# A two-stack transformer on one core: ten products without use after each norm's sum, present and left out

## The reference

```
def rmsnorm(x, g):
    y = xf * lax.rsqrt(jnp.mean(xf * xf, axis=-1, keepdims=True) + EPS)
    return (y * g).astype(x.dtype)

def hybrid_layer(x, ...):
    x = x + 0.5 * swiglu(rmsnorm(x, ffn1_norm), ffn1_wg, ffn1_wu, ffn1_wd)
    h = rmsnorm(x, mix_norm)
    proj = h @ w_in
    ...
    x = x + jnp.concatenate([na_o, gla_o], axis=-1) @ w_out
    x = x + 0.5 * swiglu(rmsnorm(x, ffn2_norm), ffn2_wg, ffn2_wu, ffn2_wd)
```

## Time and profile before

| | |
|---|---|
| median of three runs | 2177.46 us (2175.4 to 2190.49) |
| profiled execution, its own time | 2181.22 us |
| its span, first to last instruction | 2179.4 us |
| its mean granted TensorE clock | 0.979 of full speed |
| PE busy | 2119.0 us, 97% of the span |
| DVE busy | 1587.0 us, 73% |
| ACT busy | 1193.6 us, 55% |
| chain that ended last | PE 89%, DVE 5%, ACT 2%, DMA 2%, issue 1% |

### The profile page before, as it was taken

How to read it: one execution, slowest core, us unless ns; L and a number is a source line. 1 busy time by engine, 2 the same in 40 slices (tenths; PEclk the granted TensorE clock), 3 DMA queues, 4 the chain that set the end, 5 groups by cost and what they waited for, 6 DMA issues and landing times.

```text
span 2179.4 us, 32300 instructions
## 1 busy us (share of the span) xinstructions
PE 2119.0 (97%) x13054; PEld 1844.0 (85%) x13054; DVE 1587.0 (73%) x2592; ACT 1193.6 (55%) x2028; POOL 38.7 (2%) x38
## 2 busy tenths in 40 slices
PE   8999999999999999999899998999999999999998
PEld 7888998888888898888788896788888887668887
DVE  7887667887887576887688767588766665777665
ACT  6555565554654565655555447555455553555553
POOL 0002000000002000000000000000000000000000
PEclk9999999999999999999999997999999998799999
DMA  7886335775677533687477642287655454104543
GB/s 283 307 267 214 131 117 192 281 254 200 252 281 258 177 114 136 229 282 236 154 281 269 229 174 97 78 289 270 219 186 191 162 181 159 43 1 154 182 168 133
DMA packets 78092, 426.67 MB, mean 196 GB/s; under 512 B 9697, under 2 KB 10465, under 8 KB 47633
## 3 DMA queue, kind: packets, MB, share of 16 engines
q1 hardware_dynamic: 77968, 425.01, 55.9%
HBM read 423.93 MB, written 1.05 MB: 195 GB/s over the span
## 4 chain that ended last, share of the span: by engine, by line
PE 89%; DVE 5%; ACT 2%; DMA 2%; issue 1%; DVEq 0%; ACTq 0%
PE bank L454 40%; PE bank L458 21%; PE bank L436 5%; PE bank L438 4%; PE bank L437 4%; DVE slot_lo L1345 2%; PE bank L446 1%; PE bank L648 1%; DMA slot<-in_wd_dram 1%; PE bank L504 1%; PE bank L506 1%; PE bank L505 1%; PE bank L898 1%; DMA slot<-in_slots_dram 1%; ACT slot_hi L993 1%
## 5 line engine op out<-in xcount | busy, mean ns | idle before, releaser
L1345 DVE TENSOR_TENSOR slot_lo<-slot,slot_hi 128x1024 fp32r<-128x1024 f32 (+1 forms) x728 | 799.9, 1114 | 211.3 <-ACT slot_hi L993 210.0
L993 ACT ACTIVATE slot_hi<-slot 128x1024 fp32r<-128x1024 f32 (+1 forms) x728 | 678.3, 957 | 242.9 <-PE bank L454 110.8
L454 PE MATMUL bank<-h_both,slot_hi 128*128 128x512 f32 x2688 | 674.4, 392 | 0.0
L454 PEld LDWEIGHTS bank<-h_both,slot_hi 128*128 128x128 f32 x2688 | 483.5, 189 | 86.1
L458 PEld LDWEIGHTS bank<-h_both,slot_lo 128*128 128x128 f32 x2688 | 366.7, 190 | 26.3
L458 PE MATMUL bank<-h_both,slot_lo 128*128 128x256 f32 x2688 | 374.8, 282 | 0.0
L454 PE MATMUL bank<-act_both,slot_hi 128*128 128x512 f32 x1232 | 307.0, 395 | 0.0
L1040 ACT ACTIVATE room<-bank 128x512 f32<-128x512 f32 x176 | 105.1, 597 | 335.4 <-PE bank L454 335.3
L454 PEld LDWEIGHTS bank<-act_both,slot_hi 128*128 128x128 f32 x1232 | 223.7, 188 | 46.0
L1455 DVE TENSOR_TENSOR room<-room,bank 128x512 f32<-128x512 f32 x176 | 121.1, 688 | 149.7 <-ACT room L1040 149.7
L436 PE MATMUL bank<-h_both,slot_hi 128*128 128x256 f32 x736 | 213.7, 290 | 3.7 <-issue 1.0
(11 more groups left out here) (241 smaller groups left out, 2189.3 us busy)
## 6 DMA issues: line engine op xcount, KB each, us to landing
slot<-in_slots_dram SPq DMA_DIRECT2D x236, 1024.0 KB, 4.8
slot<-in_wd_dram SPq DMA_DIRECT2D x128, 704.0 KB, 4.1
room<-in_mod_w_dram SPq DMA_DIRECT2D x144, 512.0 KB, 4.9
room<-in_na_bias_dram SPq DMA_DIRECT2D x8, 512.0 KB, 6.1
x<-in_x_dram SPq DMA_DIRECT2D x1, 1024.0 KB, 5.3
out_dram<-h SPq DMA_DIRECT2D x4, 256.0 KB, 2.2
cond<-in_cond_dram SPq DMA_DIRECT2D x1, 512.0 KB, 9.8
room<-in_gla_mask_dram SPq DMA_DIRECT2D x1, 512.0 KB, 5.7
```

The source lines that it names most:

```text
L454: return pe.matmul(o, slot_hi[b][:, w:w + P], x_both.rearrange("p a b -> p (a b)"), start=first, stop=last)
L993: act.activation(slot_hi[b][:, c0:c1], slot[raw][:, c0:c1], ACT.Copy).then_inc(s["hi_ready"], 1)
L1345: ins = dve.tensor_tensor(slot_lo[b][:, c0:c1], slot[raw][:, c0:c1], slot_hi[b][:, c0:c1].bitcast(F32), ALU.subtract)
```

## The change

The constant `WARM` goes from 10 to 0, so `keep_warm` issues nothing. Nothing else differs: the loops of `WARM_START` and of eight products at the program's start stay.

```diff
         CONST_LOADS = 18
-        WARM = 10
+        WARM = 0
         WARM_START = 9
```

## The result

| | before | after |
|---|---|---|
| median of the runs | 2177.46 us (2173.7 to 2190.49, five runs) | 2200.63 us (2190.03 to 2204.59, five runs) |
| profiled execution, its own time | 2181.22 us | 2190.03 us |
| its span | 2179.4 us | 2188.2 us |
| its mean granted clock | 0.979 | 0.969 |

The ratio is 1.0082, with a 95% interval of 1.0042 to 1.0122: leaving the ten products out makes the kernel 0.8% slower, some 18 us by the ratio and 23 by the medians. The forecast was +8.4 us. The profiled execution after, 2190.0, is where the forecast had it (2189.6), but it is the fastest of its kernel's five.

What follows compares the result with a forecast made beforehand. PE, busy 97% of the span, was taken as the bound. Ten places at 0.9 us (+9.0), overruns returned (-0.6) and the ten themselves (0) gave +8.4 us: profiled 2189.6, median 2186, 8-in-10 range 2177 to 2198.

Steps and rivals of the forecast that it cites:

- the ten are off the path: Behind each sum, PE waits about 2.6 us for ACT and DVE anyway; removing the ten products there gains 0.
- The clock falls at nearly all ten: Without the ten products, the clock was expected to drop to half behind nearly all ten sums; four had it before.
- The price of one place, 0.9 us: Each first slot behind a sum loses 0.9 us to half clock; ten places add 9.0 us.
- the one bare place: Stack boundary's second sum, without products behind it before: 3.4 us of half clock under products, costing 0.71 us.
- My upper bound of 1.7 a place: Highest price per place: 3.4 us of half clock under products, with none hidden by DVE's slack.
- What I named as signs: First product 2.6 us after the sum, slow rows in four or five chunks, clock 0.974, second slot at 9.5 to 10.2 us.
- Half of the half clock: Skill's rule for throttled time: 1.7 us per 3.4 us stretch, 17 us for ten places; forecast priced it lower.
- The overruns given back, 0.6 us: Where the clock fell near four sums, the ten overran the wait; removing them returns 0.6 us in all.
- The eleventh call, 0: At the stack boundary, the ten ended 4.94 us before the next sum; removing them changes 0.
- much slower: Rival: half clock persists under dense products, one stretch giving 2198 us, two 2210; chance 0.08.
- The base: Started from the profiled execution, 2181.2 us, then took 3.7 us off the forecast to reach the runs' median.
- Within 1%: Outcome where the whole kernel's time stays within 1% (22 us) of before; chance 0.93.

Runs made afterwards that it cites:

- before, again: The kernel before, unchanged, run and traced a second time: ratio 0.9986 (0.9965 to 1.0007).
- warm_after_ffn: Against the kernel before, the ten products left out at the four mixer ends only, kept at the feed-forward ends: ratio 1.0016, median 2184.9 us.
- warm_after_mixer: Against the kernel before, the ten products left out at the seven feed-forward ends only, kept at the mixer ends: ratio 1.0053, median 2191.8 us.
- bare_again: The changed kernel, without the ten products, run again for a second trace: ratio to before 1.0074, median 2197.1 us.
- dense2_bare: Against before: ten left out, nine products added ahead of mixer 2's scores, sixteen of 512 columns ahead of mixer 3's attention; ratio 1.0109.

## Why the prediction was right, and where its sizes were not

**What bounds the kernel, and that the ten are off the path: right.** The wait between sum and first product is 2.44 to 2.66 us in the trace of after. Taking out products that had kept PE busy for 33.8 us returned nothing. (A slip of reading without effect: the page's clock has three slices below nine tenths, 7, 8 and 7, and not two.)

**The clock falls at nearly all ten: right.** It fell at ten of ten in both traces, and with products of 16 columns in their place as well.

**The price of one place, 0.9 us: too low.** It measured 1.2 to 1.5 on average. The step that was off is the length of the half clock under products. I took the 3.4 us of the one bare place; the windows show about 6.8 us at half at seven of ten in the first trace and at four in the second, where a fifth has 10.2, and up to 6.1 us of it lay under products. With 3.4 us under products the F places cost 0.5 to 1.4, near the 0.71 of the earlier trace rows; where 6 us lay under products, the price is 2.0 to 2.3. My upper bound of 1.7 a place fell with it: one bare place says nothing on how long the stretch lasts at the others, and not even at itself (5.6 us and 1.73 in the second trace of before); the bound should have allowed it to double. Ten places gave 12.0 to 14.6 us where the sum had 9.0. What I named as signs came out likewise: the first product 2.6 us behind the sum, rows of 0.63 and 0.41 us; but the mean clock fell to 0.969 and not 0.974, the slow rows went past the fifth chunk, and the second slot of the last feed-forward came at 10.5 us where I had given 9.5 to 10.2.

**Half of the half clock.** The Trainium skill ("TensorE: Matmul & The Clock Gate", section "HAM oscillation") prices throttled time at its length times 1 minus 1.2/2.4, that is half. For 3.4 us it would be 1.7, and the places with one such stretch cost 0.5 to 1.4 (that DVE's pace hides the rest is how I explain it); for the 6.1 us under products at 205 it would be 3.1, and the place cost 2.27. The rule stays an upper bound here.

**The overruns given back, 0.6 us: right and negligible.** They are the 0.2 of 1593 and less elsewhere in the first trace; in "before, again" one place (540) cost 1.1 with the ten present.

**The eleventh call, 0: right.** 9.71 and 9.77 after, 9.79 and 10.81 before.

**Mixer 3: missing from the sum.** Its attention took 78 us in one trace of the changed kernel and 92 in the other, with its clock. Both traces of before have 78; with the ten at every place, longer ones (81 to 91 us) are traced only in kernels with products added ahead of it. That the long kind is more frequent without the ten is what the spread of the single runs suggests, and not what the traces show. The whole difference is 16 to 19 us by the ratios (1.0074 to 1.0089); the places carry 12 to 15; the remaining few us are in line with this, and `warm_after_ffn` and `warm_after_mixer`, with 4.4 and 7.8 us more in mixer 3, too. I had named "much slower" for a half clock that persists, but under dense products; it persists in attention only, and the dense products brought it back after at most 6.2 us of them in every trace. Whether and why the change makes the long kind likelier is open. My two attempts to hold the clock there failed, and no run separates a cause.

**The base.** I made the sum against an execution that was 4 us longer than the second one in mixer 2's attention, and took the 3.7 us to the median off again; that was sound, and the agreement of 2190.0 with 2189.6 is luck, two errors that cancel: places 4 to 5 us dearer, a start 4 us lower.

**Chances.** "Within 1%" with 0.93 holds for the ratio, 1.0082. The median, 2200.6, lies above the upper end of 2198 that I gave; 1.0082 times 2177.5 is 2195.3, inside it. The range held with the ratio because its upper end allowed for one half clock that persists under dense products, which did not come; what filled it instead were dearer places and mixer 3.

## What to carry to other kernels

A wait of PE that the profile shows as free can still be worth filling: the price of its emptiness is the clock of the products behind it. In the first slots here, which also wait for their producer, that was 0.5 to 2.3 us for some 3 to 6 us of products at half clock, less than half of it at every place. Look at the granted clock in short windows around every wait before an operation without use is taken out, and take the price from a place that is bare already, with twice its stretch as the other bound. Half the filling did the same work here, so try fewer before none; and the single profile should be one of a typical run, since a second trace of before was 3.1 us shorter. Stretches in two traces are to be compared by their distance from the last common event, here the sum, and not by where they stand in the span.

## What the runs showed of the hardware

Ten products of 16 columns, with their weight loads, left the mean clock as low as none at all (0.970 and 0.969); with five of 512 columns the first slots were as short as with ten at eight of ten places. The clock's return differed by what ran: at the places the half clock lasted 3.4 or 6.8 us, at one place each in three traces 10.2 (at 346 in `bare_again` and in `warm_after_ffn`, at 871 in `dense2_bare`), and never over 6.2 us of it lay under dense products, while mixer 3's attention, 347 rows with PE busy for 98% of the time, stayed at half for 22 to 51 us. There each further microsecond at half cost 0.46 us (from 78.4 us at 0.86 to 91.6 at 0.72: 13.2 us more for 29 us more at half), about half. In mixer 2's attention, with PE busy for 86% of 31.9 us, the time did not follow the clock: 31.9 us at 0.73, 29.4 at 0.79 and at 0.88, 31.1 at 0.84.
